# Griffin/Fox model with a hybrid mixer and experts: the mixer's fifteen weight panels as split products by quarters

## The chip, the cores and the metric

The kernel runs on one core of a Trainium2 chip. The metric is the device time of one execution in microseconds (us); three runs were timed and the median is given. The engines are TensorE (PE, matmuls; PEld is its weight loads), VectorE (DVE), ScalarE (ACT), GpSimd (POOL) and SyncE (SP), which here issues most of the weight transfers.

## The reference

The model works on 256 tokens of width 1024. A Griffin layer, an MLP, a forgetting attention (Fox) and a second MLP come first. Then comes the hybrid mixer, which the change is about, then a layer with 32 experts (4 chosen for each token), whose weights of some 400 MB are all read. Cut to the mixer:

```python
proj = x @ w_in                       # 1024 -> 7 x 512 + 2 x 1024
sq, sk, sv, hq, hf, hi, hg, gate_sb, gate_hg = split(proj)
o_sb = stick_breaking_attention(sq, sk, sv)      # 8 heads of 64
f = lower_bound + (1.0 - lower_bound) * sigmoid(hf)
o_hg = hgrn2_recurrence(silu(hq), 1.0 - f, log(f), hi)   # 4 heads of 128
o_hg = rms_norm_per_head(o_hg) * hgrn_norm_g * sigmoid(hg)
merged = sigmoid(gate_sb) * (o_sb @ w_branch_sb) + sigmoid(gate_hg) * (o_hg @ w_branch_hgrn)
x = layer_norm(ALPHA * x + merged @ w_out)
```

All inputs and outputs are float32.

## The kernel before

Everything is written out by hand for each engine, in the order in which the engine runs it, with semaphores between the engines. The 256 tokens are two tiles (`tt`) of 128. Weights before the experts come as 61 **panels** of 128x4096 floats (2048 KB), loaded by SyncE (L273) in turn into a ring of four buffers (`panel_ring`); SyncE waits in `slot_free` until the panel four back is done with.

**Whole panels in F32.** The Griffin layer and the mixer multiply straight from the ring. Panels 46 to 60 are the mixer's: 0 q, 1 k, 2 v, 3 hq, 4 hf, 5 hi, 6 hg, 7 to 10 the gates, 11 and 12 the two branches, 13 and 14 the output (numbers within the mixer). `project_T` (L395) makes a transposed result, 128x256 at a time; `project_nat` (L404) and `gate_tile` (L1329) a natural one, 128x512 at a time; `accumulate_nat` (L418) is for panels that lie by rows. The last product of a panel adds to `consumed`.

**Split panels in F32R.** In the MLPs and in Fox each panel is taken in four quarters (128x1024). For each quarter ScalarE's `high` (L477) copies it to the type F32R, and VectorE's `low` (L484) subtracts that from the quarter, which leaves the rest, also F32R. The activations are split in the same way (`hT_high`, `hT_low`). TensorE then adds three F32R products for each chunk: high by high, high by low, low by high (`PARTS`). There are four pairs of buffers for quarters; `high` of quarter n waits until the products of quarter n - 4 are done (`part_done`), `low` waits for `high`, the products for `low`. A quarter can lie by columns (`product_T`, L503; by one token tile `product_T_tile`, L514), by two rows of chunks (`product_nat`, L526) or by one row (`product_out`, `out_tile`, L543). At the turns between these layers `turn_act` and `turn_dve` split the next layer's first quarters and the normed activations.

**The mixer.** TensorE runs: panels q, k, v; the scores of the first four heads of the attention; panel hq; their sums (`stick_sums`, L1288); panel hf; their values; the scores of the other four heads; panel hi; their sums; panel hg; their values. Then come the **levels**: the recurrence over the tokens is computed as seven levels of masked score products (`level_scores`, L1336, 8 matmuls of 128x128; the trace counts each F32 matmul as two), and behind each a half gate panel (`gate_tile`). For a level ScalarE makes `decay` (exp), GpSimd the decayed queries (`levels_pool`, L1267), VectorE the decayed keys (`decay_k`, L1557), the next difference (`decay`, L1546) and the masked copy into `hg_scores` (L1575). Then follow the cross part, the values of the recurrence (L1366 to L1368), the first branch, the norm of `o_hg`, the second branch; VectorE multiplies both branches by their gates and adds them over both token tiles at once (L1604 to L1609), TensorE transposes the sum (16 transposes, L928), VectorE copies it to `hT` (L1612), and the two output panels end the mixer. VectorE updates x by token tiles (L1618).

**What comes behind.** ScalarE then issues small late loads, router_b the last of them (L2012). SyncE's first load of expert weights (L2296) waits for all of these (`LATE_MOE`). From there the expert weights stream through their own ring.

## Time and profile before

| | us |
|---|---|
| median of 3 runs | 1915.95 (1915.81 to 1916.29) |
| the profiled execution, its own time | 1916.36 |
| its span | 1915.2 |
| mixer, first to last product | 650.38 to 907.40 |
| experts' weight stream | about 915 to 1915 |

| engine | busy us of the span |
|---|---|
| TensorE | 1777.6 (93%) |
| VectorE | 708.5 (37%) |
| ScalarE | 515.5 (27%) |
| GpSimd | 52.9 (3%) |

The page gives one profiled execution; times are counted from the start of its span. The chain that ended last is made of 67% TensorE and 24% DMA, the latter nearly all expert weights. The share that an engine is busy says little here, since the stretches have different limits; the views by stretch and the waits say more.

### The profile page before, as it was taken

The numbers are of one execution on the slowest core, as the hardware profiler recorded it, in microseconds if no ns is written. First come the engines' busy times: TensorE is split into PE (matmuls) and PEld (weight loads), VectorE is DVE, ScalarE is ACT, GpSimd is POOL, SyncE is SP. The second block draws the span as 40 slices with busy tenths as digits, with TensorE's granted clock in tenths as the row PEclk, the third lists the DMA queues.
The fourth block names the chain that finished last, engine by engine and source line by source line (L and its number), as shares of the span: only waits on it lengthen the run. The fifth ranks groups of instructions, "written<-read, shape, count | busy, mean of one in ns | idle before, by whom it ended". The sixth has DMA issues, their size and how long they took to land.

```text
span 1915.2 us, 23354 instructions
## 1 busy us (share of the span) xinstructions
PE 1777.6 (93%) x8863; PEld 1006.9 (53%) x8864; DVE 708.5 (37%) x1034; ACT 515.5 (27%) x690; POOL 52.9 (3%) x67
## 2 busy tenths in 40 slices
PE   7999999889999999998699999999999998999996
PEld 6779997688999776553333333233232332333332
DVE  3544446744454223642422232232222222222324
ACT  1545554443554123330111111111111111111111
POOL 0000000000000200410000000000000000000000
PEclk9999999989999999999699999999999998999998
DMA  7345555402455342320999999999999997899995
GB/s 254 132 176 192 202 178 176 171 7 89 180 200 192 127 142 99 121 88 0 393 367 429 428 428 428 429 428 428 428 429 428 428 429 289 360 429 428 427 430 226
DMA packets 84958, 537.02 MB, mean 280 GB/s; under 512 B 8736, under 2 KB 8840, under 8 KB 60328
## 3 DMA queue, kind: packets, MB, share of 16 engines
q1 hardware_dynamic: 79088, 531.64, 68.5%
q10 hardware_dynamic: 5816, 4.59, 0.8%
q8 instruction: 41, 0.67, 0.1%
q14 instruction: 13, 0.11, 0.0%
HBM read 535.17 MB, written 1.05 MB: 280 GB/s over the span
## 4 chain that ended last, share of the span: by engine, by line
PE 67%; DMA 24%; DVE 5%; ACT 2%; issue 1%; ACTq 0%; POOL 0%; SPq 0%; PEldq 0%; DVEq 0%; POOLq 0%
DMA expert_ring<-in_expert_w_up 24%; PE psA L1824 20%; PE psA L543 10%; PE psB L503 9%; PE psB L395 6%; PE psA L418 4%; PE psB L526 3%; PE psA L1329 3%; PE psB L404 2%; PE psB L514 1%; PE psA L1830 1%; PE psB L1853 1%; PE psB L928 1%; PE psB L1336 1%; PE psB L350 1%
## 5 line engine op out<-in xcount | busy, mean ns | idle before, releaser
L1824 PE MATMUL psA<-expert_ring,gathered_T 128*64 128x512 f32 x1024 | 455.1, 597 | 30.8 <-DMA expert_ring<-in_expert_w_up 30.8
L1825 PE MATMUL psA<-expert_ring,gathered_T 128*64 128x512 f32 x1024 | 455.1, 597 | 0.0
L1824 PEld LDWEIGHTS psA<-expert_ring,gathered_T 128*64 128x64 f32 x1024 | 135.0, 137 | 343.6 <-issue 281.0
L484 DVE TENSOR_TENSOR w_low<-panel_ring,w_high 128x1024 fp32r<-128x1024 f32 x160 | 195.0, 1224 | 167.2 <-ACT w_high L477 166.9
L1824 PE MATMUL psA<-expert_ring,activated_T 128*64 128x512 f32 x528 | 240.5, 598 | 3.1 <-ACT activated_T L2085 0.9
L1825 PE MATMUL psA<-expert_ring,activated_T 128*64 128x512 f32 x528 | 240.5, 598 | 0.0
L477 ACT ACTIVATE w_high<-panel_ring 128x1024 fp32r<-128x1024 f32 x160 | 168.2, 1057 | 203.5 <-PE psA L543 88.7
L2215 DVE TENSOR_SCALAR normed<-psA 128x512 f32<-128x512 f32 x32 | 22.1, 692 | 389.2 <-PE psA L1825 389.2
L2044 ACT ACTIVATE normed<-normed 128x512 f32<-128x512 f32 x32 | 20.1, 630 | 477.9 <-DVE normed L2215 477.9
L1824 PEld LDWEIGHTS psA<-expert_ring,activated_T 128*64 128x64 f32 x528 | 66.9, 136 | 136.1 <-issue 125.3
L2166 DVE TENSOR_TENSOR moe_sum<-moe_sum,psB 128x1024 f32<-128x1024 f32 x68 | 82.8, 1218 | 150.3 <-PE psB L1853 150.3
L503 PE MATMUL psB<-hT_high,w_high 128*128 128x256 f32 x480 | 135.9, 283 | 0.0
L503 PE MATMUL psB<-hT_high,w_low 128*128 128x256 f32 x480 | 135.8, 283 | 0.0
L503 PE MATMUL psB<-hT_low,w_high 128*128 128x256 f32 x480 | 135.8, 283 | 0.0
L1825 PEld LDWEIGHTS psA<-expert_ring,gathered_T 128*64 128x64 f32 x1024 | 135.0, 137 | 0.0
L395 PE MATMUL psB<-hT,panel_ring 128*128 128x256 f32 x512 | 113.2, 383 | 2.6 <-DVE hT L363 1.3
L395 PEld LDWEIGHTS psB<-hT,panel_ring 128*128 128x128 f32 x512 | 98.0, 192 | 16.7 <-DVE hT L365 1.7
L543 PE MATMUL psA<-w_high,aT_high 128*128 128x512 f32 x256 | 99.9, 390 | 0.0
L543 PE MATMUL psA<-w_low,aT_high 128*128 128x512 f32 x256 | 99.7, 389 | 0.0
L543 PE MATMUL psA<-w_high,aT_low 128*128 128x512 f32 x256 | 99.6, 389 | 0.0
L503 PEld LDWEIGHTS psB<-hT_high,w_high 128*128 128x128 f32 x480 | 92.1, 192 | 0.2
L503 PEld LDWEIGHTS psB<-hT_low,w_high 128*128 128x128 f32 x480 | 92.1, 192 | 0.2
(438 smaller groups left out, 2456.4 us busy)
## 6 DMA issues: line engine op xcount, KB each, us to landing
expert_ring<-in_expert_w_up SPq DMA_DIRECT2D x128, 2048.0 KB, 25.4
expert_ring<-in_expert_w_down SPq DMA_DIRECT2D x64, 2048.0 KB, 22.3
panel_ring<-in_mlp_w SPq DMA_DIRECT2D x32, 2048.0 KB, 8.0
panel_ring<-in_w_in SPq DMA_DIRECT2D x11, 2048.0 KB, 7.9
panel_ring<-in_fox_w_in SPq DMA_DIRECT2D x6, 2048.0 KB, 8.0
panel_ring<-in_lru_w_in SPq DMA_DIRECT2D x4, 2048.0 KB, 18.0
panel_ring<-in_lru_w_out SPq DMA_DIRECT2D x2, 2048.0 KB, 7.9
panel_ring<-in_fox_w_out SPq DMA_DIRECT2D x2, 2048.0 KB, 8.4
```

What stands on the lines that cost most here:

```text
L395: last = M.matmul(out[:, m, :], w[:, c, m * P:(m + 1) * P], k.hT[:, c, :], start=(c == 0), stop=(c == KD - 1))
L404: last = M.matmul(ps[:, tt, :], k.hT[:, c, tt * P:(tt + 1) * P], w[:, c, :], start=(c == 0), stop=(c == KD - 1))
L418: mm = M.matmul(k.psA[:, 2 * tt + half, :], aT[:, c, tt * P:(tt + 1) * P], w[:, c, half * 512:(half + 1) * 512], start=first and c == 0, s ...
L477: A.activation(part_rows(k.w[n % BUFFERS][0], view), view, ACT.Copy).then_inc(s.w_high, 1)
L484: V.tensor_tensor(w[1], view, w[0].bitcast(F32), ALU.subtract).then_inc(s.w_low, 1)
L503: last = k.nc.tensor.matmul(out, w[a][:, c, :], h[b][:, c, :], start=(c == 0 and a == b), stop=(c == KD - 1 and a == 1))
L526: last = k.nc.tensor.matmul(ps[:, tt, :], h[a][:, 2 * i + c, tt * P:(tt + 1) * P], w[b][:, c, :], start=(i == 0 and c == 0 and a == b), st ...
L543: last = k.nc.tensor.matmul(k.psA[:, 2 * tt + half, :], a_parts[a][:, tt * P:(tt + 1) * P], w[b][:, half * 512:(half + 1) * 512], start=(f ...
L1329: last = M.matmul(ps[:, tt, :], k.hT[:, c, tt * P:(tt + 1) * P], wj[:, c, :], start=(c == 0), stop=(c == KD - 1))
L1824: M.matmul(ps[0:SLOTS], lhsT, rhs[0], **flags)
L1825: return M.matmul(ps[SLOTS:P], lhsT, rhs[1], **flags)
L2166: return V.tensor_tensor(m.acc[:, tt, :], m.acc[:, tt, :], flat(m.S[:]), ALU.add)
```

## The change

All fifteen mixer panels now take the split path, each in four quarters, with `high`, `low` and three F32R products.

- Kinds of quarters: q, k, hq, hf by columns; v, hi, hg and the four gate panels by two rows; the branches and the output by one row. The first two quarters of q are multiplied by token tiles.
- The turn from the second MLP to the mixer now uses `turn_act` and `turn_dve`, so the first panel's four quarters and the activations are split there.
- `slot_free` of all panels from 6 on is the last `low` of the panel, also for the expert loads that reuse the space.
- The lows stand on VectorE, and the highs on ScalarE, among the mixer's own work, at places written out by hand (`lows(m0, m1)`, `highs(m0, m1)`, quarters counted through the mixer). `stick_weights` is split in two; the attention's sums of the second half, the first decays and `stick_out(1)` stand in a new order among them.
- The gate of the recurrence's output (`sig_g`) is multiplied by the gain inside the levels; `o_hg` is then multiplied by one tensor of 128x1024 fewer.
- The last part goes by token tiles: the gates are applied, added (`merge`), transposed (`merged_T`) and split (`merged_high`, `merged_low`) a tile at a time, and the second branch and both output panels are multiplied a tile at a time.
- Several tiles share memory to make room for the split buffers: `o_sb` and `o_hg` with the normed x, `sig_g` and `hg_v` with `hT`, the masks with the cross tile, the gain with the gates.
- `levels_pool` is as before, but for one wait on `hq_ready`. GpSimd still makes the decayed queries.

The diff, cut to its core:

```diff
-    return (k.s.w_low, part_of(p, 3) + 1) if SPLIT <= p < WHOLE else (k.s.consumed, whole_done(p))
+    return (k.s.w_low, part_of(p, 3) + 1) if p >= SPLIT else (k.s.consumed, p + 1)
...
-def product_out_last(k, p, a_parts_of, between):
+def product_out_tiles(k, p, a_parts_of, first, last, after):
 
 
     s, w = k.s, []
@@ -554,13 +546,13 @@
         for i in range(4):
             if tt == 0:
                 w.append(split_part(k, p, i))
-            last = out_tile(k, w[i], a_parts_of(i), tt, False, i == 3)
+            mm = out_tile(k, w[i], a_parts_of(i), tt, first and i == 0, last and i == 3)
             if tt == TT - 1:
-                last.then_inc(s.part_done, 1)
-                if i == 0:
-                    between()
-        if tt == 0:
-            last.then_inc(s.out_first, 1)
+                mm.then_inc(s.part_done, 1)
+            elif last and i == 3:
+                mm.then_inc(s.out_first, 1)
+            if (tt, i) in after:
+                after[tt, i]()
...
-        for tt in range(TT):
-            update(tt)
-            hT_dve(k, 4, tt, None)
+        turn_dve(k, 4, None, update, (HYBRID, BY_COLUMNS))
...
+HYBRID_KINDS = [BY_COLUMNS] * 2 + [BY_TWO_ROWS] + [BY_COLUMNS] * 2 + [BY_TWO_ROWS] * 6 + [BY_ROW] * 4
...
-    M.wait_ge(s.hT_ready, 10)
-    project_T(k, HYBRID, k.psB[0])
-    project_T(k, HYBRID + 1, k.psB[1])
+    q = lambda i: by_four(k.psB[0])[:, i, :]
+    M.wait_ge(s.h_low, TT * 3 + 1)
+    product_T_tile(k, HYBRID, 0, q(0), 0)
+    product_T_tile(k, HYBRID, 1, q(1), 0)
+    M.wait_ge(s.h_low, TT * 3 + 2)
+    product_T_tile(k, HYBRID, 0, q(0), 1)
+    product_T_tile(k, HYBRID, 1, q(1), 1)
+    for i in (2, 3):
+        product_T(k, HYBRID, i, q(i))
+    project_T(1, k.psB[1])
...
-    def gate_tile(n):
-        j, tt = n // 2, n % 2
-        ps, wj = k.psA[:, 2 * (j % 2):2 * (j % 2) + 2, :], k.panel(HYBRID + 7 + j, KD)
-        M.wait_ge(*arrived(k, HYBRID + 7 + j))
-        if j < 2:
+    def gate_half(n):
+        j = n // 2
+        if n == 0:
             M.wait_ge(s.o_sb_ready, 2)
-        else:
+        elif n >= 4 and n % 2 == 0:
             M.wait_ge(s.gates_copied, j - 1)
-        for c in range(KD):
-            last = M.matmul(ps[:, tt, :], k.hT[:, c, tt * P:(tt + 1) * P], wj[:, c, :], start=(c == 0), stop=(c == KD - 1))
-        if tt:
-            last.then_inc(s.consumed, 1)
+        for i in (2 * (n % 2), 2 * (n % 2) + 1):
+            product_nat(k, HYBRID + 7 + j, i, k.psA[:, 2 * (j % 2):2 * (j % 2) + 2, :])
...
+    parts = h_parts(k)
+    row = lambda c: [part[:, c, :] for part in parts]
+    M.wait_ge(s.gates_copied, 4)
     M.wait_ge(s.sb_T, 1)
-    M.wait_ge(s.gates_copied, 4)
-    accumulate_nat(k, HYBRID + 11, h.oT[0], True, True)
+    for i in range(4):
+        product_out(k, HYBRID + 11, i, row(i), i == 0, i == 3)
     M.wait_ge(s.hg_normed, 1)
     transpose_pe(k, h.o_hg, 0, 4, k.psB[0], k.ident[:])
+
+    def merged_T(tt):
+        rows_T_pe(k, tt, h.gates[:, 0], (s.merged, tt + 1)).then_inc(s.nat_T, 1)
+
     M.wait_ge(s.sb_T, 2)
     M.wait_ge(s.branch_read, 1)
-    accumulate_nat(k, HYBRID + 12, h.oT[1], True, True)
-    M.wait_ge(s.merged, 1)
-    for g in range(2):
-        transpose_pe(k, h.gates[:, 0], 4 * g, 4, k.psB[g], k.ident[:])
-    M.wait_ge(s.nat_evicted, 8)
-    M.wait_ge(s.branch_read, 2)
-    accumulate_nat(k, HYBRID + 13, k.hT[:, 0:4, :], True, False)
-    accumulate_nat(k, HYBRID + 14, k.hT[:, 4:8, :], False, True)
+    product_out_tiles(k, HYBRID + 12, lambda i: row(4 + i), True, True, {
+        (0, 3): lambda: M.wait_ge(s.branch_read, 2),
+        (1, 2): lambda: merged_T(0)})
+    M.wait_ge(s.nat_evicted, 7)
+    product_out_tiles(k, HYBRID + 13, row, True, False, {
+        (0, 2): lambda: merged_T(1),
+        (0, 3): lambda: M.wait_ge(s.nat_evicted, 8)})
+    product_out_tiles(k, HYBRID + 14, lambda i: row(4 + i), False, True, {})
...
+    highs(4, 8)
+    A.wait_ge(*hybrid_done(s, 0))
+    A.activation(h.qT[:], by_four(k.psB[0]), ACT.Copy, scale=HD ** -0.5).then_inc(s.evicted, 1)
+    highs(8, 16)
+    A.wait_ge(*hybrid_done(s, 2))
...
     decay(0)
+    highs(28, 32)
+    A.wait_ge(*hybrid_done(s, 6))
+    A.activation(h.sig_g, k.psB[0][:], ACT.Sigmoid).then_inc(s.evicted, 1)
     decay(1)
-    copy_gate(0)
-    decay(2)
-    decay(3)
-    copy_gate(1)
-    decay(4)
-    decay(5)
-    copy_gate(2)
-    decay(6)
-    decay(7)
-    copy_gate(3)
-    A.wait_ge(s.nat_T, 7)
-    A.activation(h.oT[0], by_four(k.psB[0]), ACT.Copy).then_inc(s.sb_T, 1)
+    for l in range(LEVELS + 1):
+        highs(32 + 2 * l, 33 + 2 * l)
+        if l + 2 <= LEVELS:
+            decay(l + 2)
+        highs(33 + 2 * l, 34 + 2 * l)
+        if l % 2:
+            copy_gate(l // 2)
+    branch_high(0, 7)
     A.wait_ge(s.hg_out, 3)
-    A.activation(h.o_hg[:], k.psB[1][:], ACT.Copy).then_inc(s.o_hg_copied, 1)
+    A.activation(h.o_hg, k.psB[1][:], ACT.Copy).then_inc(s.o_hg_copied, 1)
     A.wait_ge(s.hg_var, 1)
     A.activation(v.st[:, 1], v.st[:, 0], ACT.Sqrt).then_inc(s.hg_root, 1)
-    A.wait_ge(s.gates_copied, 4)
-    for i in range(2):
-        g2 = h.gates[:, i].rearrange("p t n -> p (t n)")
-        A.activation(g2, g2, ACT.Sigmoid).then_inc(s.gate_sig, 1)
-    A.wait_ge(s.nat_T, 8)
-    A.activation(h.oT[1], by_four(k.psB[0]), ACT.Copy).then_inc(s.sb_T, 1)
+    highs(48, 49)
+    gate_sigmoid(0)
+    highs(49, 51)
+    gate_sigmoid(1)
+    branch_high(1, 8)
+    highs(51, 53)
+    merged_high(0)
+    highs(53, 55)
+    merged_high(1)
+    highs(55, 60)
...
+    lows(24, 28)
+    V.wait_ge(s.log_f, 1)
+    for hd in range(HGH):
+        V.tensor_tensor_scan(h.hb[:, hd], h.keep, h.hb[:, hd], 0.0, ALU.mult, ALU.add).then_inc(*dve.step())
+    stick_log_weights(1)
+    V.wait_ge(*dve.last())
+    decay(0)
+    stick_weights(1)
+    lows(28, 30)
+    V.wait_ge(s.hk_ready, 1)
+    V.wait_ge(s.hq_ready, 1)
+    scale(0)
+    decay(1)
+    lows(30, 32)
+    stick_out(1)
+    V.wait_ge(s.o_sb_ready, 2)
+    V.wait_ge(s.hg_out, 1)
+    V.tensor_tensor(v.S[:], level_out(k.psB[1]), k.ident[:].unsqueeze(1).to_broadcast([P, HGH * TT, P]),
+                    ALU.mult).then_inc(s.level_read, 1)
+    for l in range(LEVELS + 1):
+        if l < LEVELS:
+            scale(l + 1)
+        if l + 2 == LEVELS:
+            V.wait_ge(s.late, 112)
+            V.wait_ge(s.evicted, E1 + 5)
+            V.tensor_tensor(h.sig_g, h.sig_g, h.gn.unsqueeze(1).to_broadcast([P, TT, HGW]), ALU.mult).then_inc(*dve.step())
+        if l + 2 <= LEVELS:
+            decay(l + 2)
+        if l:
+            take_level(l - 1)
+        lows(32 + 2 * l, 34 + 2 * l)
     V.wait_ge(s.hg_out, 2)
-    V.tensor_copy(v.X[:], k.psB[1][:, 0, :].rearrange("p (h t) -> p h t", t=P)).then_inc(s.level_read, 1)
+    V.tensor_copy(v.X, k.psB[1][:, 0, :].rearrange("p (h t) -> p h t", t=P)).then_inc(s.level_read, 1)
+    branch_low(0)
...
+    lows(48, 51)
+    gate = lambda i, tt: h.gates[:, i, tt, :]
+    psum = lambda tt: flat(k.psA[:, 2 * tt:2 * tt + 2, :])
+    V.wait_ge(*hybrid_done(s, 11))
     V.wait_ge(s.gate_sig, 2)
-    V.tensor_tensor(g2[0], g2[0], psf, ALU.mult).then_inc(s.branch_read, 1)
-    V.wait_ge(s.consumed, BEFORE_HYBRID + 13)
+    for tt in range(TT):
+        V.tensor_tensor(gate(0, tt), gate(0, tt), psum(tt), ALU.mult).then_inc(s.branch_read, 1)
+    branch_low(1)
+    lows(51, 52)
+
+    def merge(tt):
+        V.tensor_tensor(gate(1, tt), gate(1, tt), psum(tt), ALU.mult).then_inc(*dve.step())
+        V.wait_ge(*dve.last())
+        V.wait_ge(s.branch_read, tt + 1)
+        V.tensor_tensor(gate(0, tt), gate(0, tt), gate(1, tt), ALU.add).then_inc(s.merged, 1)
+
     V.wait_ge(s.out_first, OUT["branch_hgrn"])
-    V.tensor_tensor(g2[1], g2[1], psf, ALU.mult).then_inc(s.branch_read, 1)
-    V.wait_ge(s.branch_read, 2)
-    V.tensor_tensor(g2[0], g2[0], g2[1], ALU.add).then_inc(s.merged, 1)
-    for g in range(2):
-        V.wait_ge(s.nat_T, 9 + g)
-        V.tensor_copy(k.hT[:, 4 * g:4 * g + 4, :], by_four(k.psB[g])).then_inc(s.nat_evicted, 1)
+    merge(0)
+    lows(52, 53)
+    merged_low(0)
+    lows(53, 54)
+    V.wait_ge(*hybrid_done(s, 12))
+    merge(1)
+    lows(54, 55)
+    merged_low(1)
+    lows(55, 60)
```

Where the instructions now stand, at three places of VectorE's queue (names with a number are buffers; `w0_low` to `w3_low` are written by `low`, each for one quarter). **Ahead of the levels**, from the weights of the attention's second half (`sb_w`) to the first scores. Before:

```order
L1502 TENSOR_TENSOR sb_w_81<-sb_w_81,sb_mask_74 128x1536
L1532 SCALAR_TENSOR_TENSOR hg_cum_log_f_72<-scan_keep_76,hg_cum_log_f_72 128x256 x4
L1508 COPY o_sb_63<-psA 128x4x2x64
L1546 TENSOR_TENSOR decay_82<-hg_cum_log_f_72 128x1024
L1557 TENSOR_TENSOR k_decayed_84<-hg_k_71,decay_82 128x1024
L1546 TENSOR_TENSOR sb_kT_padded_68<-hg_cum_log_f_72 128x1024
L1566 TENSOR_TENSOR hg_scores_85<-psB1,ident_5 128x1024
```

After (`normed_10` holds `o_sb` now):

```order
L1624 SCALAR_TENSOR_TENSOR hg_cum_log_f_69<-masks_then_cross_70,hg_cum_log_f_69 128x256 x4
L1545 TENSOR_TENSOR log_w_74<-log_w_74,psA 128x1536
L1566 TENSOR_TENSOR decay_76<-hg_cum_log_f_69 128x1024
L1549 TENSOR_TENSOR sb_w_75<-sb_w_75,masks_then_cross_70 128x1536
L476 TENSOR_TENSOR w0_low_13<-panel_ring_11,w0_high_12 128x1024
L476 TENSOR_TENSOR w1_low_15<-panel_ring_11,w1_high_14 128x1024
L1577 TENSOR_TENSOR k_decayed_78<-hg_k_68,decay_76 128x1024
L1566 TENSOR_TENSOR sb_kT_padded_65<-hg_cum_log_f_69 128x1024
L476 TENSOR_TENSOR w2_low_17<-panel_ring_11,w2_high_16 128x1024
L476 TENSOR_TENSOR w3_low_19<-panel_ring_11,w3_high_18 128x1024
L1555 COPY normed_10<-psA 128x4x2x64
L1638 TENSOR_TENSOR hg_scores_79<-psB1,ident_5 128x1024
```

Four lows and the first decayed keys stand between `sb_w` and the copy of the attention's output, which was directly behind the scans.

**One period of the levels**, on VectorE. Before, two levels:

```order
L1557 TENSOR_TENSOR sb_kT_padded_68<-hg_k_71,sb_kT_padded_68 128x1024
L1546 TENSOR_TENSOR decay_82<-hg_cum_log_f_72 128x1024
L1575 COPY_PREDICATED hg_scores_85<-level_masks_75,psB0 128x1024
L1557 TENSOR_TENSOR k_decayed_84<-hg_k_71,decay_82 128x1024
L1546 TENSOR_TENSOR sb_kT_padded_68<-hg_cum_log_f_72 128x1024
L1575 COPY_PREDICATED hg_scores_85<-level_masks_75,psB1 128x1024
```

After, one level and the start of the next:

```order
L1577 TENSOR_TENSOR k_decayed_78<-hg_k_68,decay_76 128x1024
L1566 TENSOR_TENSOR sb_kT_padded_65<-hg_cum_log_f_69 128x1024
L1586 COPY_PREDICATED hg_scores_79<-level_masks_71,psB0 128x1024
L476 TENSOR_TENSOR w2_low_17<-panel_ring_11,w2_high_16 128x1024
L476 TENSOR_TENSOR w3_low_19<-panel_ring_11,w3_high_18 128x1024
L1577 TENSOR_TENSOR sb_kT_padded_65<-hg_k_68,sb_kT_padded_65 128x1024
L1566 TENSOR_TENSOR decay_76<-hg_cum_log_f_69 128x1024
L1586 COPY_PREDICATED hg_scores_79<-level_masks_71,psB1 128x1024
```

Two lows have come in behind each masked copy; the three other instructions of a level keep their order.

**The end of the mixer**, on VectorE, from the gate of the recurrence's output to the update of x. Before:

```order
L1598 TENSOR_TENSOR o_hg_64<-o_hg_64,sigmoid_hg_66 128x1024
L1604 TENSOR_TENSOR gates_65<-gates_65,psA 128x2048
L1607 TENSOR_TENSOR gates_65<-gates_65,psA 128x2048
L1609 TENSOR_TENSOR gates_65<-gates_65 128x2048
L1612 COPY hT_2<-psB0 128x1024
L1612 COPY hT_2<-psB1 128x1024
L1618 SCALAR_TENSOR_TENSOR x_1<-x_1,psA 128x1024 x2
```

After, as far as the second tile's activations (`hT_low_21`):

```order
L1678 TENSOR_TENSOR gates_63<-gates_63,psA 128x1024 x2
L1591 TENSOR_TENSOR hT_low_21<-psB0,hT_high_20 128x1024
L476 TENSOR_TENSOR w3_low_19<-panel_ring_11,w3_high_18 128x1024
L1683 TENSOR_TENSOR gates_63<-gates_63,psA 128x1024
L1686 TENSOR_TENSOR gates_63<-gates_63 128x1024
L476 TENSOR_TENSOR w0_low_13<-panel_ring_11,w0_high_12 128x1024
L1596 TENSOR_TENSOR hT_low_21<-psB0,hT_high_20 128x8x128
L476 TENSOR_TENSOR w1_low_15<-panel_ring_11,w1_high_14 128x1024
L1683 TENSOR_TENSOR gates_63<-gates_63,psA 128x1024
L1686 TENSOR_TENSOR gates_63<-gates_63 128x1024
L476 TENSOR_TENSOR w2_low_17<-panel_ring_11,w2_high_16 128x1024
L1596 TENSOR_TENSOR hT_low_21<-psB1,hT_high_20 128x8x128
```

The three passes of 128x2048 are now six of 128x1024, with lows between them, and the copies to `hT` have become subtractions that leave the low part.

## Rows read from the trace of the kernel before

**Rows 1.** A table by stretch; the first line names its columns (us, instructions).

```profile
core 0: us, PE busy (x) PEld busy (x) DVE busy (x) ACT busy (x) POOL busy (x), PEclk, DMA share, GB/s
770.00:836.00 66.00, 65.75 (x242) 36.22 (x241) 41.71 (x24) 18.07 (x19) 25.46 (x8) 1.00 0.27 96
...
950.00:1915.00 965.00, 891.77 (x4299) 302.65 (x4298) 265.46 (x543) 152.24 (x264) 0.00 (x0) 0.99 0.96 405
```

**Rows 2.** SyncE's waits: total us, number, longest.

```profile
SPq L2296 <- DMA router_b<-in_router_b: 61.7, 1, 61.7
```

**Rows 3.** The chain that ended last, in order of time: start, us, engine and line.

```profile
745.79 0.43 PE psA L1288 x2
...
749.30 13.73 PE psB L404 x32
...
776.68 6.87 PE psA L1329 x16
783.54 1.78 PE psB L1336 x16
...
870.26 2.30 DVE gates L1607
...
910.04 5.54 DMA router_b<-in_router_b
```

**Rows 4.** Timeline of TensorE: start, us, line, [idle before, releaser].

```profile
460.05 1.09 PE L350 MATMUL psB<-ident,x 128*128 128x128 f32 x8 [1.31 <-DVE x L442]
...
650.38 27.89 PE L395 MATMUL psB<-hT,panel_ring 128*128 128x256 f32 x128 [1.32 <-DVE hT L363]
...
856.25 13.97 PE L418 MATMUL psA<-panel_ring,hg_v 128*128 128x512 f32 x32 [1.55 <-ACT hg_v L1466]
...
874.93 3.42 PE L928 MATMUL psB<-ident,gates 128*128 128x128 f32 x16 [4.71 <-DVE gates L1609]
879.67 27.73 PE L418 MATMUL psA<-panel_ring,hT 128*128 128x512 f32 x64 [1.32 <-DVE hT L1612]
```

**Rows 5.** Table by stretch, columns of rows 1: three stretches of F32R products.

```profile
510.75:533.79 23.04, 23.04 (x194) 23.04 (x193) 10.94 (x9) 11.39 (x11) 0.00 (x0) 1.00 0.50 183
318.64:329.50 10.86, 10.86 (x49) 9.01 (x48) 8.75 (x8) 5.14 (x6) 0.00 (x0) 1.00 0.58 198
460.89:466.20 5.31, 5.31 (x51) 5.31 (x49) 4.95 (x5) 3.14 (x5) 0.00 (x0) 1.00 0.01 3
```

**Rows 6.** The page's costliest groups: busy us, mean ns, then idle before.

```profile
L484 DVE TENSOR_TENSOR w_low<-panel_ring,w_high 128x1024 fp32r<-128x1024 f32 x160 | 195.0, 1224 | 167.2 <-ACT w_high L477 166.9
...
L477 ACT ACTIVATE w_high<-panel_ring 128x1024 fp32r<-128x1024 f32 x160 | 168.2, 1057 | 203.5 <-PE psA L543 88.7
```

**Rows 7.** Timelines of VectorE (DVE) and GpSimd (POOL), columns of rows 4.

```profile
742.75 1.76 DVE L1496 TENSOR_TENSOR softplus<-softplus,sb_mask 128x1536 f32<-128x1536 f32 x1
...
765.70 0.69 DVE L1508 COPY o_sb<-psA 128x512 f32<-128x512 f32 x1 [8.95 <-PE psA L940]
...
771.14 1.23 DVE L1557 TENSOR_TENSOR k_decayed<-hg_k,decay 128x1024 f32<-128x1024 f32 x1 [3.49 <-ACT decay L1434]
772.28 3.37 DVE L1546 TENSOR_TENSOR sb_kT_padded<-hg_cum_log_f 128x1024 f32<-128x1024 f32 x1
...
771.19 3.38 POOL L1267 TENSOR_TENSOR q_decayed<-hg_q,decay 128x1024 f32<-128x1024 f32 x1 [109.23 <-ACT decay L1434]
...
826.77 1.77 POOL L1267 TENSOR_TENSOR sb_qT<-hg_q,sb_kT_padded 128x512 f32<-128x512 f32 x1 [2.06 <-ACT sb_kT_padded L1436]
```

**Rows 8.** Table by stretch, columns of rows 1: the granted clock around waits.

```profile
380.00:384.40 4.40, 0.92 (x5) 0.52 (x3) 4.33 (x4) 0.00 (x0) 0.00 (x0) 0.50 0.85 337
384.40:388.00 3.60, 3.56 (x12) 3.20 (x13) 0.00 (x0) 0.00 (x0) 0.00 (x0) 0.50 0.00 0
...
870.00:875.00 5.00, 0.29 (x2) 0.07 (x2) 4.58 (x2) 0.00 (x0) 0.00 (x0) 0.95 0.00 0
875.00:878.40 3.40, 3.35 (x16) 3.12 (x16) 1.24 (x2) 0.00 (x0) 0.00 (x0) 0.56 0.00 0
```

246 lines of the change are left out of this document (126 added, 120 removed).

## The prediction

> **What bounds the kernel now.** The table by stretch comes first. The reader should see two regimes: in the levels of the recurrence TensorE is busy 65.75 of 66.00 us, and from 950 us on the DMA engines are 0.96 busy at 405 GB/s, so the experts run at the pace of their weights [rows 1]. The second question is when that stream may start. SyncE's list of waits answers: its first expert load stands 61.7 us on the semaphore of the late loads, router_b the last of them [rows 2]. The chain shows the same step: router_b is in transit from 910.04 for 5.54 us [rows 3], right behind the mixer's last products, which end at 907.40 [rows 4], one update of x by VectorE and three issues by ScalarE. So whatever the mixer saves up to that update moves the stream and the end by as much, and nothing behind it gives it back. Inside the mixer the chain is nearly all TensorE; VectorE is busy 41.71 of 66.00 us in the levels, so it has room, but not much [rows 1].
>
> **The sum, part a: TensorE's products.** Before, in F32: the first two panels 27.89 us [rows 4], so a column panel (q, k, hq, hf) takes 13.94 and four take 55.7; three natural panels of 13.73 make 41.2 [rows 3]; eight half gate panels of 6.87 make 55.0 [rows 3]; of the four row panels the second takes 13.97 and the last two 27.73 [rows 4], with 13.7 for the first 55.4. Together 207.3.
> After, each quarter is three F32R products per chunk, and the MLP and the Fox mixer of this trace already run all three forms. Two column panels stand in a window of 23.04 us: eight quarters of 2.88. Four quarters by two rows stand in 10.86: 2.72 each; a row quarter has as many products of the same 512 columns. Forty-eight products on 128 columns (a column quarter of one panel, by token tile) take 5.31, 0.11 each [rows 5]. The mixer has 60 quarters: 2 by token tile (10.6), 14 by columns (40.3), 44 by two rows or by rows (119.7), together 170.6. **a = −36.7.**
>
> **b. The turn from the MLP.** Today the first product waits 1.32 us for VectorE's hT [rows 4]. The same turn between Fox and MLP has its split pieces ready: its transposes wait 1.31 for x and take 0.84 to 460.89, where the products begin at once [rows 4, 5]. The mixer now turns in that way. **b = −1.3.** The eight highs and lows of panel 46 sit in the turn on idle engines.
>
> **c. New waits.** A low takes 1.22 us, a high 1.06 [rows 6], and lows on VectorE follow each other every 1.14 us, as 771.14 to 772.28 shows [rows 7]. 60 of each less the turn's four are 56 x 1.14 = 64 us on VectorE. While TensorE has 11 us of a panel they hide. The ring of four panels isn't pressed either: a slot comes free with the last low of its panel, and the DMA engines are 0.27 busy in the levels [rows 1]. They don't hide where VectorE works for TensorE's next step:
> 1. stick_sums(1) reads softplus, ready at 744.51 [rows 7]; TensorE got there at 745.79 [rows 3], 1.2 late. The panel ahead is now 2.85 shorter (13.73 − 10.88): +1.6.
> 2. gate_half(0) waits for stick_out(1). In order VectorE has, behind stick_weights(1): two lows (2.3), scale (1.1), decay(1) held by GpSimd's product (2.2 + 1.1, below), two lows (2.3), stick_out (0.7) [rows 7]: 9.7. TensorE has meanwhile the last quarter of panel 6 (some 2.5 of it), the values (2.67, from 763.03 to 765.70 [rows 3, 7]) and the first scores (1.78 [rows 3]): 6.9. +2.8.
> 3. The copy X waits behind the low of quarter 47, whose high waits for gate_half(7): 1.06 + 1.22 + 0.69 and a hand-over of 0.2, 3.2. TensorE has the cross products and eight transposes, half of what takes 1.78 and 1.7 elsewhere: 1.8. +1.4.
> 4. Before the second branch VectorE reads the first through the gate in two halves (870.26 2.30 for the whole [rows 3], so 1.15 each) and writes branch_low (1.22), with two hand-overs 3.9; today's wait there is 1.55 [rows 4]. +2.4.
> 5. The merge by tiles: today TensorE waits 4.71 and 1.32 [rows 4]. Now the transposes of tile 0 lie inside the second branch and cost 1.2 (high 1.06, low 1.22, a hand-over 0.3, less the half quarter of 1.36 that TensorE runs meanwhile); then 1.9, since the low of quarter 54 stands behind merge(1); then 3.7 (high 1.06, merged_low 1.22, low of 55 1.22, a hand-over). 6.8 against 6.03: +0.8.
> **c = +9.0.** VectorE's and ScalarE's durations come from rows of the same shape; the hold by GpSimd in item 2 is the unknown among them, 2.2 or 3.4, and is weighed next. If none of the waits came, c would be −7.6 (today's 1.55 and 6.03 gone); with the longer hold it is +10.2. I take +9.0, since each wait follows from instructions in a fixed order.
>
> **d. Short starts that go.** The 16 transposes behind the 4.71 us wait take 3.42 [rows 4] in a stretch of granted clock 0.56 [rows 8]: the 1.2 GHz level; at 2.4 GHz 1.7. They are now in two eights behind short waits. With small restarts **d = −2.0.**
>
> **The levels.** The period was 1.78 + 6.87 = 8.65 [rows 3]; TensorE now needs 1.78 + 2 x 2.72 = 7.2. VectorE runs scale, decay, take_level and two lows: 5 x 1.14 and what GpSimd holds it. Today decay (772.28) lasts 3.37, where a product of the same shape that runs ahead of GpSimd lasts 1.23 (771.14), and it ends as GpSimd's product does (771.19 + 3.38) [rows 7]: one waits for the other. Two readings: GpSimd needs 2.2 itself and stood behind the VectorE instruction that began 0.05 before it (3.38 − 1.18), or it holds VectorE for 3.38. With half the columns it takes 1.77 [rows 7]: taking off a VectorE instruction of half size (0.65) leaves 1.12, half of 2.2; the other reading needs a fixed 0.16, which is possible. I take 2.2, because the instruction at 771.14 lies wholly inside GpSimd's and isn't held, while the next is. Then VectorE needs 7.9 a level, 0.7 more than TensorE. By the laying below, the lows enter the levels 3.5 ahead, and the five full levels between the first and the last use that up. 0 for the levels, and no room left.
> The Trainium skill, page "SBUF — State Buffer", section "Who interferes with whom", says the port pair of VectorE and GpSimd is an exclusive lock held for a whole instruction; the 3.37 above agrees. "GPSIMD Engine Reference", section on performance versus the Vector engine, gives 4497 ns for 2048 elements; half, an estimate of 2.25, would favour the first reading (sum −31.0 instead of −23.3).
>
> **Sum:** −36.7 − 1.3 + 9.0 − 2.0 = −31.0. Laying all instructions of the mixer in the new order on these durations gives −30.6 (the old order laid so gives 256.8 us from first to last product, the trace 257.0); I take −30.6.
> **e. The clock.** At 870–875 a wait of 4.71 left 0.95, and the next 3.4 us ran at 0.56. TensorE was busy 0.92 of the 4.40 us before 384.40, and the stretch from there ran at 0.50 [rows 8]; after 1.55 at 856.25 nothing slowed (13.97 against 13.73) [rows 4]. The new waits of 2.8, 3.9 and 3.7 lie between. The last one follows 1.9 and little work, like 384.40. I count one fall, 4 us at half speed: **+2.1**.
> **Result −28.5.** Against the profiled run's 1916.36 that is 1887.9; the median shown is 0.4 lower: **1887.5 us**.
>
> **Rivals.**
> A2, waits cheaper: no fall of the clock and one or two waits hidden, −31 to −34, 1883 to 1885. For: nothing fell after 1.55. Against: three waits near 4.
> B, GpSimd holds VectorE for the whole 3.38: VectorE needs 9.1 a level, 1.9 more than TensorE; six levels 11.2, less 3.5 ahead, +7.7: −30.6 + 7.7 + 2.1 = −20.8, **1895.1**. For: in every full-size pair the row is 3.38, whoever was ahead. Against: the unheld instruction at 771.14.
> C, slower: in the levels the quarters chain. A high waits for its buffer of four, the low for the high, the product for the low, and scale for the low. If no step overlaps, a level costs 7.2 + 2 x 1.06 + 7.9 = 17.3; eight cost 81 more: +52, 1968. It decides from a period of 7.2 + 28.5/8 = 10.8. Against: four buffers are two levels of lead.
> D, no change: the experts' start is not tied to the mixer, 1915.9. Against: the 61.7 us wait.
>
> **How the numbers follow.** Forecast (with a us or two on one wait, 1885–1890) 0.66; A2 0.10; B with half measures of it (1890–1898) 0.17; C 0.04; D 0.03. The range covers forecast, A2 and B's centre: 1883 to 1895.5. A measurement of this kernel tells some 0.2% (3.8 us) from no change. Faster 0.93, same 0.03, slower 0.04.
>
> **What would show it.** Quarters of 2.88 and 2.72; level period 7.2 with VectorE at 7.9 (B: over 8.5, TensorE waiting for w_low each level); waits of 1.6, 2.8, 1.4, 3.9, 1.2, 1.9 and 3.7 at the named places; the granted clock below 1 once, before the output panels; last update of x at 879, first expert loads at 887, and 965 us of experts as before. It is wrong if quarters wait in panels 1 to 6, or if the stretch behind 950 changes its length.

## The result and the profile after

The changed kernel takes 1888.68 us (median of 4 runs, 1886.02 to 1892.68), the kernel before 1915.88 (4 runs, 1912.23 to 1916.29). The ratio is 0.9864, with a 95% interval of 0.9841 to 0.9887. That is 27.2 us less by the medians, where 28.5 were forecast; 1888.7 lies inside the range of 1883 to 1895.5 and within its own smaller one of 1885 to 1890.

The page and the table by stretch of the changed kernel (us, busy us and instructions of PE, PEld, DVE, ACT and POOL, granted clock, DMA share, GB/s), which answer to [rows 1]:

```profile
PE 1746.0 (92%) x9215; PEld 1044.9 (55%) x9216; DVE 779.4 (41%) x1101; ACT 579.1 (31%) x754; POOL 51.6 (3%) x66
...
765.00:825.00 60.00, 58.76 (x336) 51.21 (x335) 51.09 (x40) 32.21 (x32) 14.72 (x6) 1.00 0.30 106
...
922.00:1888.00 966.00, 894.67 (x4306) 303.62 (x4306) 266.35 (x544) 153.50 (x265) 0.00 (x0) 0.99 0.96 407
```

In the levels VectorE has gone from 41.71 busy of 66.00 us [rows 1] to 51.09 of 60.00, and TensorE still has hardly a gap. The experts' stretch is what it was: 966 us at 0.96 of the DMA engines. Its start hangs on the same load. SyncE's longest wait (total us, number, longest), and the chain that ended last, in order of time (start, us, engine and line), answer to [rows 2, 3]:

```profile
SPq L2383 <- DMA router_b<-in_router_b: 73.3, 1, 73.3
```

```profile
649.51 10.67 PE psB L506 x96
660.18 17.33 PE psB L495 x144
677.51 10.91 PE psB L518 x48
...
765.72 1.78 PE psB L1348 x16
767.50 5.48 PE psA L518 x24
772.98 1.78 PE psB L1348 x16
...
883.90 1.23 DVE x L1703
...
886.50 5.65 DMA router_b<-in_router_b
```

The reader should check the terms of the sum here. The two quarters by token tile take 10.67 (forecast 10.6); six quarters by columns take 17.33, 2.89 each (2.88); the v panel takes 10.91 (10.88); half a gate panel takes 5.48 (5.44), and a level 7.26 (7.2), in place of 8.65. In the chain the mixer runs from 649.51 (its first product starts at 649.27) to 883.9, where it ran from 650.38 to 907.40: its last product comes 23.5 us earlier.

TensorE's waits in the mixer, from its timeline (start, us, line, and in brackets the idle time before and what ended it):

```profile
736.39 0.70 PE L1297 MATMUL psA<-softplus,after__8 128*128 128x256 f32 x2 [1.61 <-DVE softplus L1541]
...
758.34 0.50 PE L518 MATMUL psA<-w_high,hT_high 128*128 128x512 f32 x1 [2.80 <-DVE normed L1555]
...
819.49 0.49 PE L1375 MATMUL psB<-hT,hg_scores 128*128 128x128 f32 x2 [1.24 <-DVE masks_then_cross L1653]
...
837.98 0.74 PE L535 MATMUL psA<-w_high,hT_high 128*128 128x512 f32 x1 [3.76 <-DVE hT_low L1591]
...
852.65 0.50 PE L535 MATMUL psA<-w_high,hT_high 128*128 128x512 f32 x1 [1.00 <-DVE hT_low L1596]
...
857.30 0.50 PE L535 MATMUL psA<-w_high,hT_high 128*128 128x512 f32 x1 [1.64 <-DVE w_low L476]
...
863.34 0.80 PE L535 MATMUL psA<-w_high,hT_high 128*128 128x512 f32 x1 [3.50 <-DVE w_low L476]
```

These are the seven waits of part c, in order of time. They were forecast as 1.6, 2.8, 1.4, 3.9, 1.2, 1.9 and 3.7. They answer to [rows 4], whose 4.71, 1.55 and 1.32 are gone.

The granted clock behind the three long ones, from the table by stretch, answers to [rows 8]:

```profile
758.34:765.70 7.36, 7.36 (x26) 5.92 (x27) 6.43 (x4) 3.28 (x4) 2.38 (x1) 0.77 0.78 285
837.98:849.24 11.26, 11.26 (x43) 9.10 (x44) 4.75 (x4) 1.06 (x1) 0.00 (x0) 0.85 0.00 1
863.34:869.40 6.06, 6.06 (x16) 4.82 (x16) 0.00 (x0) 0.48 (x1) 0.00 (x0) 0.55 0.02 3
```

In each TensorE is busy all the time and part of it runs at the 1.2 GHz level. The chain gives the price:

```profile
758.34 7.38 PE psA L518 x24
...
837.98 11.42 PE psA L535 x42
...
863.34 20.54 PE psA L535 x78
```

The first half gate panel takes 7.38 in place of 5.48 (1.9). The 42 products take 11.42, where an estimate from the 5.48 for 24 gives 9.5 to 9.6 (1.9). The 78 products take 20.54, and took 18.03 in e4 below, where the clock stayed up (2.5). Three falls cost 6.3 us, where one of 2.1 was forecast.

GpSimd and VectorE in the levels, from their timelines, answer to [rows 7]:

```profile
782.98 2.40 POOL L1255 TENSOR_TENSOR q_decayed<-hg_q,decay 128x1024 f32<-128x1024 f32 x1 [5.62 <-ACT decay L1437]
```

```profile
778.37 1.21 DVE L1577 TENSOR_TENSOR sb_kT_padded<-hg_k,sb_kT_padded 128x1024 f32<-128x1024 f32 x1
...
783.88 2.58 DVE L476 TENSOR_TENSOR w_low<-panel_ring,w_high 128x1024 fp32r<-128x1024 f32 x1 [0.84 <-ACT w_high L469]
786.38 1.21 DVE L1577 TENSOR_TENSOR k_decayed<-hg_k,decay 128x1024 f32<-128x1024 f32 x1
```

The new order shows GpSimd's product alone for once: 2.40, not 3.38. VectorE's low that begins inside it takes 2.58 in place of 1.22 and ends 1.08 after it. VectorE's period is 786.38 − 778.37 = 8.0 (forecast 7.9), more than TensorE's 7.26; TensorE waits nowhere all the same, because VectorE's lead at the start was large enough. The 8.0 isn't VectorE's work alone: ahead of that low it stands idle for 0.84, waiting for ScalarE's high, and then it is held for 1.36 (2.58 − 1.22). Both lie inside GpSimd's 2.40.

### The profile page after: what moved, and what is told of

Its sections match the earlier page's. It is cut to its first block, busy times and chain, and to the rows that moved or that the text cites. A ratio compares the mean times of both kernels' runs of the same rounds, so it can differ in the third digit from the quotient of the medians.

```text
span 1889.0 us, 24202 instructions
## 1 busy us (share of the span) xinstructions
PE 1746.0 (92%) x9215; PEld 1044.9 (55%) x9216; DVE 779.4 (41%) x1101; ACT 579.1 (31%) x754; POOL 51.6 (3%) x66
## 4 chain that ended last, share of the span: by engine, by line
PE 63%; DMA 26%; DVE 6%; ACT 3%; issue 2%; ACTq 0%; SPq 0%; PEldq 0%; POOL 0%; DVEq 0%; POOLq 0%
DMA expert_ring<-in_expert_w_up 25%; PE psA L1911 19%; PE psA L535 12%; PE psB L495 11%; PE psB L518 3%; PE psB L387 3%; PE psA L518 2%; PE psB L506 2%; PE psA L410 1%; DVE w_low L476 1%; PE psA L1917 1%; PE psB L342 1%; PE psB L1940 1%; PE psB L1348 1%; PE psA L982 1%
## 5 line engine op out<-in xcount | busy, mean ns | idle before, releaser
L476 DVE TENSOR_TENSOR w_low<-panel_ring,w_high 128x1024 fp32r<-128x1024 f32 x220 | 275.2, 1258 | 202.9 <-ACT w_high L469 202.0
L469 ACT ACTIVATE w_high<-panel_ring 128x1024 fp32r<-128x1024 f32 x220 | 230.2, 1056 | 269.8 <-PE psA L535 112.8
L495 PE MATMUL psB<-hT_high,w_high 128*128 128x256 f32 x592 | 167.8, 283 | 0.0
L495 PE MATMUL psB<-hT_low,w_high 128*128 128x256 f32 x592 | 167.5, 283 | 0.0
L495 PE MATMUL psB<-hT_high,w_low 128*128 128x256 f32 x592 | 167.5, 283 | 0.0
L495 PEld LDWEIGHTS psB<-hT_low,w_high 128*128 128x128 f32 x592 | 113.6, 192 | 0.2
L495 PEld LDWEIGHTS psB<-hT_high,w_high 128*128 128x128 f32 x592 | 113.6, 192 | 0.2
L495 PEld LDWEIGHTS psB<-hT_high,w_low 128*128 128x128 f32 x592 | 113.6, 192 | 0.0
L2150 ACT ACTIVATE expert_out_high<-psA,gate_of_slot 128x512 fp32r<-128x512 f32 x32 | 22.0, 687 | 231.2 <-PE psA L1912 231.2
```

The costliest lines, as they stand in the source:

```text
L469: A.activation(part_rows(k.w[n % BUFFERS][0], view), view, ACT.Copy).then_inc(s.w_high, 1)
L476: V.tensor_tensor(w[1], view, w[0].bitcast(F32), ALU.subtract).then_inc(s.w_low, 1)
L495: last = k.nc.tensor.matmul(out, w[a][:, c, :], h[b][:, c, :], start=(c == 0 and a == b), stop=(c == KD - 1 and a == 1))
L2150: A.activation(m.y[0][:], m.DN, ACT.Copy, scale=m.slot_gate[:]).then_inc(s.y_copied, 1)
```

## The experiments

The runs e1 to e4, e7 and e8 start from the changed kernel and make one edit each; the others put edits together. All are measured by the mixer's time, from the start of its first product to the end of its last in the profiled run: 234.6 us in the changed kernel (its first record at 649.27, its last end at 883.87), 257.0 before. That interval says more than the whole time: from the last product to the end of the span the thirteen profiled runs took between 1004.1 and 1009.1 us, with the same code there. "Laid" means that all instructions of the mixer are laid in their order with the durations of rows. The changed kernel laid so takes 227.7: 257.0 less the prediction's 30.6, of which 1.3 lie ahead of the first product. The measured 234.6 less 6.3 for the clock is 228.3. No view shows a laying; it is a forecast, to be judged by what was measured. (The expectations count the third fall as 2.9; the 18.03 wasn't known then.) Each trace is one execution, so a wait or a fall of the clock read from it is shown for that execution.

### One wait at a time

**e1, the attention's output first.** The wait of 2.80 stands before gate_half(0), the first half gate panel. VectorE now takes the attention's output (`stick_out(1)`) ahead of one decay and two lows.

```diff
     scale(0)
+    stick_out(1)
     decay(1)
     lows(30, 32)
-    stick_out(1)
```

> From the changed kernel, VectorE takes the attention's second output (stick_out) right behind the first decayed keys, ahead of one decay and two lows. Nothing is left out. In the changed kernel TensorE waits 2.8 us there and its clock falls for some 3 us behind it, which costs 1.9 more. Theory 1 (VectorE has no lead left in the levels, since GpSimd's product holds it 1.4 us in each): the wait goes, but comes back inside the levels, spread over several places; without the clock the mixer, 234.4 us from first to last product, gets only 0.2 shorter, and the fall of the clock (1.9) goes: 232.3. Theory 2 (each wait is its own price, the levels have room): the mixer gets 2.8 + 1.9 shorter, 229.7.

Measured: mixer 232.36, median 1888.62 against 1916.32 (ratio 0.9848, 0.9824 to 0.9871), and so no different from the changed kernel's 1888.68. TensorE's waits, from its timeline:

```profile
797.37 0.91 PE L1348 MATMUL psB<-sb_qT,sb_kT_padded 128*128 128x128 f32 x6 [0.17 <-DVE hg_scores L1586]
...
806.29 0.91 PE L1348 MATMUL psB<-q_decayed,k_decayed 128*128 128x128 f32 x6 [1.37 <-DVE hg_scores L1586]
...
817.64 0.49 PE L1375 MATMUL psB<-hT,hg_scores 128*128 128x128 f32 x2 [1.75 <-DVE masks_then_cross L1653]
```

The wait of 2.80 is gone, and 0.17, 1.37 and 0.5 (1.75 against 1.24) have come up later, behind VectorE's masked copies, and 0.14 at the transposes. Theory 1 had 232.3. Two falls of the clock are left, 2.7 and 1.3 by the time of their stretches; without them it is 228.4, the same as the changed kernel's 228.3. The wait was worth nothing by itself; what the edit gained in the mixer is clock.

**e2, the order of the tail.** The transposes of the merged tiles stand one half quarter earlier, and the high and low of quarter 55 ahead of those of the second tile's activations.

```diff
-        (1, 2): lambda: merged_T(0)})
+        (1, 1): lambda: merged_T(0)})
...
-        (0, 2): lambda: merged_T(1),
+        (0, 1): lambda: merged_T(1),
...
-    highs(53, 55)
+    highs(53, 56)
     merged_high(1)
-    highs(55, 60)
+    highs(56, 60)
...
-    lows(54, 55)
+    lows(54, 56)
     merged_low(1)
-    lows(55, 60)
+    lows(56, 60)
```

> From the changed kernel, the transposes of the merged tiles stand one half quarter earlier in TensorE's order, and the high and low of quarter 55 ahead of those of the second tile's activations. Nothing is left out. Theory 1 (the waits of 1.0, 1.6 and 3.5 us come from the order alone, and the fall of the clock, 2.9 us over the output panels, from the last of them): waits of 0, 0.6 and 0, no fall, the mixer 5.9 + 2.9 shorter, 225.6 us. Rival (the clock falls anyway, since TensorE had waited 3.8 before the second branch): 5.9 shorter, 228.5.

Measured: mixer 226.0, median 1878.65 (ratio 0.981, 0.9785 to 0.9835). Of the last part's three waits one of 0.39 is left:

```profile
835.99 0.79 PE L535 MATMUL psA<-w_high,hT_high 128*128 128x512 f32 x1 [3.76 <-DVE hT_low L1591]
...
852.82 1.09 PE L342 MATMUL psB<-ident,gates 128*128 128x128 f32 x8 [0.39 <-DVE gates L1686]
```

The clock stays at 1.00 over the output panels. Theory 1 holds (225.6). Item 5 of part c had priced the order right; another order of the same instructions is 8.6 us cheaper, 5.8 of it in these waits and 2.5 in the fall of the clock that went with the last of them.

**e3, the first branch by token tiles.** TensorE, ScalarE and VectorE change order together; TensorE's part:

```diff
-    for i in range(4):
-        product_out(k, HYBRID + 11, i, row(i), i == 0, i == 3)
-    M.wait_ge(s.hg_normed, 1)
-    transpose_pe(k, h.o_hg, 0, 4, k.psB[0], k.ident[:])
+    def o_hg_T():
+        M.wait_ge(s.hg_normed, 1)
+        transpose_pe(k, h.o_hg, 0, 4, k.psB[0], k.ident[:])
+
+    product_out_tiles(k, HYBRID + 11, row, True, True, {(1, 1): o_hg_T})
```

> From the changed kernel, the first branch goes by token tiles too, the transposes of o_hg stand inside it, and the gate is applied to its first tile while the second is multiplied. Nothing is left out. Theory 1: the wait of 3.8 before the second branch falls to 0.5, and so does the clock's fall behind it (1.9): the mixer 4.4 + 1.9 shorter, 228.1 us, with the waits of the last part as they are. Rival (the waits behind it grow, since the four buffers of quarters are held until the second tile): 1 to 3 shorter.

Measured: mixer 228.4, median 1884.17 (ratio 0.9828, 0.9806 to 0.985). The wait before the second branch is 0.18:

```profile
838.02 0.50 PE L535 MATMUL psA<-w_high,hT_high 128*128 128x512 f32 x1 [0.18 <-DVE w_low L476]
```

Theory 1 had 228.1, but this agreement is in part luck of the clock. The clock fell at 720, which wasn't forecast (told below), and before the output panels, 1.7 and 1.4 by the time of the stretches, and it stayed up behind the wait of 2.79 at 759. Without its falls the mixer is 225.3, so the edit itself brought 3.0 (from 228.3), where 4.4 was forecast; the falls cost 3.1 here and 6.3 in the changed kernel.

### GpSimd's part

**e4, the decayed queries on VectorE.**

```diff
         V.tensor_tensor(v.K[l % 2][:, :, kc], h.hk[:, :, kc], e[:, :, kc], ALU.mult).then_inc(s.k_decayed, 1)
+        qc = decayed_columns(l)[0]
+        V.tensor_tensor(v.Q[l % 2][:, :, qc], h.hq[:, :, qc], e[:, :, qc], ALU.mult).then_inc(s.q_decayed, 1)
```

> From the changed kernel, VectorE makes the decayed queries itself, GpSimd none. Nothing is left out. Theory 1 (GpSimd's product takes 2.4 us and holds VectorE for about 1.4 of a level): VectorE gains 1.4 and pays 1.14 a level, the wait before the first gate panel falls from 2.8 to 2.0, the mixer is 1.1 shorter, 233.3, or 231.4 if the clock doesn't fall behind a wait of 2.0. Rival (GpSimd's help is worth its 2.4 us, VectorE becomes the bound of the levels): TensorE waits 0.5 to 1 in each level, the mixer 4 to 8 longer.

Measured: mixer 231.7, median 1888.35 (ratio 0.9855, 0.9833 to 0.9877). TensorE waits nowhere in the levels, though VectorE now does GpSimd's work too; the wait before gate_half(0) is 2.54, more than the 2.0 laid. The rival is out. VectorE's period is 7.79 (the starts of its two differences, 777.69 and 785.48), 0.2 less than the 8.0: the hold is gone, an instruction has come in, and the wait for ScalarE's high is still there:

```profile
782.07 1.22 DVE L476 TENSOR_TENSOR w_low<-panel_ring,w_high 128x1024 fp32r<-128x1024 f32 x1 [0.83 <-ACT w_high L469]
```

In the median nothing moves, and that fits: the levels were bound by TensorE before and after. The clock fell at 720 and 836, 1.7 each, and not before the output panels, whose 78 products took 18.03 in the chain:

```profile
861.89 18.03 PE psA L535 x78
```

Without the falls the mixer is 228.3, so the 1.1 laid didn't come, and that 231.7 meets the forecast is luck of the clock.

**e9, the edits of e1 and e4 together.**

> From the changed kernel, two edits alone: the attention's output first (which by itself got the mixer 0.2 shorter beside the clock) and the decayed queries on VectorE (1.1). Nothing is left out. Theory 1 (GpSimd's hold on VectorE in the levels is why the wait of 2.8 came back there): together they bring 2.9 where one by one they bring 1.3: 224.8 without the clock, 229.5 to 231 with the two or three falls of the tail and the branch, and no wait in the levels. Rival (the two only add up): 226.4 without the clock, waits of 1.4 and 1.8 at the end of the levels as in the first experiment.

Measured: mixer 229.14, median 1887.83 (ratio 0.9856, 0.9838 to 0.9873). No wait in the levels; of those at their end only that at the cross part is left:

```profile
815.01 0.49 PE L1368 MATMUL psB<-hT,hg_scores 128*128 128x128 f32 x2 [1.42 <-DVE masks_then_cross L1648]
```

The clock fell twice, 1.9 and 1.5 by the time of the stretches; without that it is 225.7 (224.8 laid). Counted in this way e1 alone brought nothing (228.4), e4 alone nothing (228.3), and both together 2.6. The waits say the same: the 2.80 is gone, and the one at the cross part is 0.18 longer. That is theory 1, more clearly than forecast. The medians of four runs don't show it (1887.83 against 1888.62 and 1888.35); it is a reading of the mixer's interval alone.

### What stands behind TensorE

**e8, two products of three.** The helper `split_part` chooses `PARTS` without its middle member for the mixer's panels; all waits stay. In the quarters by columns this leaves out high weights by low activations, as the expectation says. In the quarters by rows, where the activations come first, it leaves out low weights by high activations. The number of products is the same.

> From the changed kernel, the mixer's products leave out high weights by low activations, so that two products of three stay; everything else runs. Part of the computation is left out. It tells what is behind TensorE: a third of its products, 56.9 us of 170.6, is gone. Theory 1 (VectorE needs 8 us a level and is next): the levels don't go below a period of 8 us against TensorE's 5.4, waits open at the attention too, and the mixer comes to 200 us plus the falls of the clock, so only half of the 57 us is gained. Rival (VectorE's lows have room everywhere): some 178 us plus the falls.

Measured, in one run: mixer 212.0, the whole 1869.17. A third of the products is gone, 56.9 us, and 22.6 are gained. The levels, from TensorE's timeline:

```profile
771.56 0.50 PE L519 MATMUL psA<-w_high,hT_high 128*128 128x512 f32 x1 [0.56 <-DVE w_low L476]
...
775.13 1.13 PE L1349 MATMUL psB<-q_decayed,k_decayed 128*128 128x128 f32 x8 [1.46 <-DVE hg_scores L1587]
...
779.57 0.50 PE L519 MATMUL psA<-w_high,hT_high 128*128 128x512 f32 x1 [0.56 <-DVE w_low L476]
783.13 1.13 PE L1349 MATMUL psB<-sb_qT,sb_kT_padded 128*128 128x128 f32 x8 [1.46 <-DVE hg_scores L1587]
```

From 771.56 to 779.57 a level takes 8.01, which is VectorE's period in the changed kernel; TensorE now waits 2.0 of it. The expectation had 200 without the clock. The granted clock was at 0.5 in six stretches, with 26.6 us of products in them; half of that, an estimate of 13, leaves 199. Theory 1 holds: behind TensorE's 7.26 stands VectorE with 8.0, so in the levels, in this order of instructions, a faster TensorE pays nothing once the lead is used up. The 8.0 holds the wait for ScalarE's high here too (0.84); e6 below takes it out. Rival C of the prediction is answered here too: even with TensorE waiting in each level, the quarters overlap and the period is 8.0, not 17.3.

### The merge

**e7, the merge over both tiles, as before.** TensorE's part of the edit:

```diff
-        (0, 3): lambda: M.wait_ge(s.branch_read, 2),
-        (1, 2): lambda: merged_T(0)})
-    M.wait_ge(s.nat_evicted, 7)
-    product_out_tiles(k, HYBRID + 13, row, True, False, {
-        (0, 2): lambda: merged_T(1),
-        (0, 3): lambda: M.wait_ge(s.nat_evicted, 8)})
+        (0, 3): lambda: M.wait_ge(s.branch_read, 2)})
+    merged_T(0)
+    merged_T(1)
+    M.wait_ge(s.nat_evicted, 8)
+    product_out_tiles(k, HYBRID + 13, row, True, False, {})
```

> From the changed kernel, the merge of the two branches is undone to the old manner: both tiles are merged when the second branch is done, then all 16 transposes, then the output panels. Nothing is left out. Theory 1 (the merge by tiles as it stands only spreads the wait): TensorE waits 2.8, 1.5 and 2.6 us instead of 1.0, 1.6 and 3.5, and the mixer stays within 1.5 us of 234.6. Rival (the merge by tiles hides half of the work): 3 us or more longer.

Measured: mixer 235.38, median 1892.54 (ratio 0.9872, 0.9857 to 0.9887). Three waits again:

```profile
853.32 0.88 PE L342 MATMUL psB<-ident,gates 128*128 128x128 f32 x6 [2.57 <-DVE gates L1684]
855.71 0.69 PE L342 MATMUL psB<-ident,gates 128*128 128x128 f32 x2 [1.30 <-DVE gates L1684]
860.05 0.80 PE L535 MATMUL psA<-w_high,hT_high 128*128 128x512 f32 x1 [2.37 <-DVE hT_low L1594]
```

They sum to 6.24, those of the changed kernel to 6.14. The mixer is 0.8 longer, and that is the clock: TensorE ran 14.2 us of the mixer at the 1.2 GHz level, where it ran 12.3 in the changed kernel, and half of the difference is 1.0. So merging by token tiles brought nothing in the order that the change gave it; e2 shows that the same tiles in another order bring 8.6.

### Together

**e5, the edits of e1 to e4. e6, those and two more:** the sums of the attention's second half behind the first quarter of panel 6, and in the levels both highs ahead of the next decay on ScalarE. **e10:** e6 with the queries back on GpSimd. **e11:** e6, and the high and low of quarter 47 behind the copy of the cross part; VectorE's part of that:

```diff
-        lows(32 + 2 * l, 34 + 2 * l)
+        lows(32 + 2 * l, 34 + 2 * l - (l == LEVELS))
     V.wait_ge(s.hg_out, 2)
     V.tensor_copy(v.X, k.psB[1][:, 0, :].rearrange("p (h t) -> p h t", t=P)).then_inc(s.level_read, 1)
     branch_low(0)
+    lows(47, 48)
```

> The edits of the four runs before, together: attention's output first, the tail's order, the first branch by tiles, VectorE makes the decayed queries. Nothing is left out. Theory 1 (VectorE's lead in the levels is what kept the first edit from paying; with GpSimd out of its way the wait of 2.8 goes for good): the mixer, 234.6 us in the changed kernel, comes to 215.5 with no fall of the clock and 217.4 with one; about 18 us below the changed kernel's 1888.7, near 1871. Rival (the gains overlap, each moved wait comes back at the next place): not under 221, 1876.

> The four edits, and two more: the attention's second sums stand behind the first quarter of panel 6 (today TensorE waits 1.6 for them), and in the levels ScalarE makes both highs ahead of the next decay. Nothing is left out. Theory 1: the wait of 1.6 goes and nothing takes its place: mixer 214.1 without and 216.0 with one fall of the clock, 1.4 below the four edits. Rival (VectorE, with six instructions a level, becomes the bound once the start is earlier): waits in the levels of 0.5 to 2, no gain over the four edits.

> From the six-edit kernel, GpSimd makes the decayed queries again. Nothing is left out. Theory 1 (once TensorE starts the levels earlier, GpSimd's hold costs time on the path): waits of 0.8, 0.4 and 2.0 at the end of the levels where the six-edit kernel has none but 1.2, the mixer 1.6 longer, 217.2. Rival (the levels still have room, GpSimd's help is free): within 0.5 of 215.6.

> The six edits, and the high and low of quarter 47 stand behind the copy of the cross part and the split of the attention's output, which no longer wait for the last gate product. Nothing is left out. Theory 1: the wait of 1.2 at the cross part goes, and nothing takes its place: the mixer 1.6 shorter than with six edits, 214.0; the median about 1869.6. Rival (the low of quarter 47 is then late for the first branch's fourth quarter): within 0.3 of the six edits.

| kernel | mixer, us | median, us | ratio to before, 95% interval |
|---|---|---|---|
| changed | 234.6 | 1888.68 | 0.9864 (0.9841 to 0.9887) |
| e5, four edits | 216.5 | 1874.59 | 0.9778 (0.9761 to 0.9795) |
| e6, six edits | 215.6 | 1871.20 | 0.9767 (0.9754 to 0.9781) |
| e10, e6 with GpSimd | 217.6 | 1874.65 | 0.9784 (0.9765 to 0.9802) |
| e11, seven edits | 214.3 | 1870.55 | 0.9762 (0.9748 to 0.9776) |

In the traces of these four the clock doesn't fall in the mixer at all. e5 came out at its laid time plus 1.0 (216.5 against 215.5 laid), e6 at plus 1.5: its sums don't wait, but before gate_half(0) it waits 0.75, which the laying hadn't. So the fifth and sixth edit brought 0.9, where 1.4 was forecast. The sixth does more for VectorE than the mixer's time tells. No low waits for a high in the full levels any more, and VectorE's period is 6.87, less than TensorE's 7.24; here are two of its differences:

```profile
780.67 1.23 DVE L1564 TENSOR_TENSOR sb_kT_padded<-hg_cum_log_f 128x1024 f32<-128x1024 f32 x1
...
787.54 1.23 DVE L1564 TENSOR_TENSOR decay<-hg_cum_log_f 128x1024 f32<-128x1024 f32 x1
```

With GpSimd back in e10 the period is 7.9, since the hold is then 2.2 (the decayed keys take 3.38 at 781.88). e10 waits 0.69 and 1.75 at the end of the levels and is 2.0 longer in the mixer (1.6 forecast); GpSimd's help costs time as soon as TensorE is early enough. e11 loses the wait at the cross part and is 1.3 shorter than e6 in the mixer (1.6 forecast), which the medians can't tell. It is the fastest kernel here, 18 us below the changed one; TensorE's longest wait between its first and last product is 0.78:

```profile
720.44 0.70 PE L1282 MATMUL psA<-sb_qT,sb_kT_padded 128*128 128x256 f32 x2 [0.78 <-DVE normed L1554]
...
831.25 0.50 PE L535 MATMUL psA<-w_high,hT_high 128*128 128x512 f32 x1 [0.18 <-DVE w_low L476]
```

## Why the prediction was right, point by point

- **Part a**, −36.7: the sizes are right to 2%. Each quarter by columns took 2.88 or 2.89, those by two rows 2.73 or 2.74, and the row quarters of the output 2.77 (18.03 for six and a half), where 2.72 stood.
- **Part b**, −1.3: −1.1 (650.38 to 649.27). The products do begin with no wait behind the transposes, but the transposes began 0.45 later than before.
- **Part c**, +9.0: the seven waits sum to 15.6 where 16.5 were laid; today's 1.55 and 6.03 are gone as said. c came to +8.0. The place and size of each was right to 0.3.
- **Part d**, −2.0: not measured by itself. Without the clock's falls the mixer is 28.7 shorter (257.0 to 228.3); c's +8.0 leaves −36.7 for a and d together, where the two had −38.7. Which of them is short by 2.0 isn't shown, and c's 1.0 hid half of it. So the laying, at 227.7, was met to 0.6 with help of opposite errors.
- **The levels**, 0: right, TensorE waited nowhere. GpSimd's product measured 2.40 alone (2.2 had been taken), VectorE's period 8.0 (7.9). The working took the time beyond VectorE's five instructions as hold by GpSimd alone. 0.84 of it is a wait for ScalarE's high, which the prediction doesn't have. It lies inside GpSimd's product, so the sum came out; but it stays when GpSimd is taken away (7.79 in e4), and goes when ScalarE makes both highs first (6.87 in e6). "No room left" held for this order: in e1, whose period is 8.0, what TensorE gained in front of the levels came back in them. Rival B falls with the 2.40. Its "whoever was ahead" was a misreading: in the trace before, VectorE's instruction began 0.04 to 0.05 ahead of GpSimd's in each full-size pair. The page "SBUF — State Buffer" of the Trainium skill, section "Who interferes with whom", says that the one of the two that issues first gets the shared ports for its whole instruction and the other is blocked; the low of 2.58 at 783.88 agrees. The estimate of 2.25 from the Trainium skill's page "GPSIMD Engine Reference", section "Performance versus the Vector engine", is 0.15 under the 2.40 measured.
- **Part e**, +2.1: mis-sized. The three waits over 2.5 us each brought a fall of the clock, 1.9 + 1.9 + 2.5 = 6.3. This is the step that failed: the working named all three waits as candidates and then took one. With it the forecast would have been 1891.7.
- **The rest**: the last product came 23.5 us earlier where 28.5 were forecast (the last update of x began at 883.9, not 879), but the span was 26.2 shorter. The other 2.6 lie behind the mixer: 1007.8 us before, 1005.1 after. The same code took 1004.1 to 1009.1 in the other traces, e5 (1009.1) and e6 (1004.1) being the ends, so a gain of the change isn't shown there. That the median came out at 1888.7, 1.2 from the forecast, is in part luck: in the profiled runs the mixer's end fell 5.0 short, and what lies behind it made up for half.
- **Rivals**: C (quarters chained in the levels) didn't come near, 7.26 against 10.8; D is out by the expert loads, which moved with the mixer. A2 is out: no wait was hidden.

## What to carry to other kernels

Where an order is fixed by hand, lay all instructions with the durations that the trace has for the same shapes; here that gave every new wait to 0.3 us before a run. Then count the clock separately, and give every wait of 2.5 us or more between products its price, a fall included (14 of 17 had one here). When an engine's period has come out right, look in its timeline at what fills it: here a wait for a third engine stood hidden in it. A wait that an engine with no lead causes can't be removed alone: e1 took away 2.8 us and got nothing but clock, until the lead behind it was made larger.

## What the runs showed of the chip

**The clock.** In the mixers of the changed kernel and of e1 to e4, e7 and e9, TensorE waited between 2.5 and 3.8 us at 17 places; in 14 cases the granted clock fell to 0.5 during the wait or within 2 us behind it, for 3.4 us in eleven of them, for 6.8 in two and for 10.2 in one; in 3 it didn't. e4 has one of these three, its 3.50 before 862, from the table by stretch:

```profile
858.00:862.00 4.00, 0.50 (x5) 0.26 (x4) 2.35 (x2) 1.97 (x2) 0.00 (x0) 1.00 0.00 0
862.00:866.00 4.00, 4.00 (x18) 3.27 (x19) 0.00 (x0) 0.96 (x1) 0.00 (x0) 1.00 0.02 4
```

Waits of 1.0 to 1.8 brought none in these kernels; in e8 the clock fell behind two in a row, 1.96 and 1.75 at 801 to 803. And behind the wait of 0.78 at 720 the clock fell in e3 and e4, and in none of the nine other kernels whose program is the same up to there; e3's stretches:

```profile
720.00:722.00 2.00, 1.56 (x6) 1.36 (x7) 1.86 (x3) 0.46 (x1) 0.00 (x0) 0.71 0.63 159
722.00:724.00 2.00, 2.00 (x8) 1.73 (x7) 1.67 (x2) 0.00 (x0) 0.00 (x0) 0.50 1.04 404
```

In both the fall behind the next long wait stayed out. What decides between such cases stays open; no run here was made to tell. The fall also began late at times: after the wait of 2.80 the first five products of the changed kernel still ran at full pace and then seven at half.

**GpSimd beside VectorE.** A product of 128x1024 takes 2.40 us on GpSimd alone and 1.23 on VectorE; the lows, VectorE instructions with two operands in SBUF, that begin inside it are held until it is done (2.58 in place of 1.22, ending 1.08 behind it). How much is lost depends on what VectorE would have done meanwhile: the hold was 1.36 where VectorE had to wait for ScalarE first, and 2.2 in e10, where it hadn't. Moving GpSimd's eight products to VectorE, which seemed to have no room, cost nothing (e4) and made the levels shorter where they were on the path (e10 against e6, 2.0 us).
